# Gated linear attention on one core: products of even and odd heads issued in turn instead of one parity after the other

## The chip, the cores and the metric

The kernel runs on 1 core of one Trainium2 chip. The metric is the device time of one execution in microseconds (us); smaller is better. Engines are named as the profile names them: PE is TensorE (PEld its weight loads), DVE is VectorE, ACT is ScalarE, POOL is GpSimd, SP is SyncE.

## The reference, cut to what matters

The program is two transformer blocks in one launch. The change touches one stage of the first block: the output of the chunked gated linear attention (GLA). Per chunk of 64 tokens, per direction (forward and backward) and per head (4 heads, 64 key columns, 128 value columns):

```
q_dec = qi * exp(b);  k_inv = ki * exp(-b)
scores = where(mask, einsum("bihk,bjhk->bhij", q_dec, k_inv), 0)
o = einsum("bhij,bjhv->bihv", scores, vi) + einsum("bihk,bhkv->bihv", q_dec, state)
```

`o` of both directions is added, normalised per head and multiplied by a gate. All of it is float32.

## The kernel before

The kernel is written out by hand: each engine has its own list of stages, and between two stages stands a `fence` (L213), at which every engine waits until all have arrived. So a stage costs what its slowest chain costs, and stages do not overlap. The order of instructions on each engine is that of the Python loops; nothing reorders the program.

The stages around the change are, in order: `pe_dec` (decayed queries and keys, transposed), `pe_states` (L1056, the state of each of the 12 chunks, then `each_states`, whose recurrence L1079 runs on DVE alone), `pe_glao` (the stage that is changed), `pe_turn` (L1161, 32 transposes) and the output projection `pe_lin` (L506).

Sequence is 512 tokens, that is four token tiles t of 128 tokens (two chunks each). What `pe_glao` does for one tile, where par is the parity of the head (h = 2 q + par, q = 0, 1) and d the direction:

- **Scores** (L1098). `kiT` and `qdT` hold keys and queries with the 64 columns of even heads on partitions 0 to 63 and those of odd heads on partitions 64 to 127. So a score product contracts over 64 rows: the upper half of the array for par 0, the lower for par 1. Group g = 2 d + par writes bank g, two products (q) each; 8 products a tile.
- **Masks** (L1129, DVE). Four multiplications, one per group, take the scores out of banks 0 to 3 into `SM`.
- **Values** (L1110). For each head and direction one product over the whole array (128 rows, 128 columns): 8 a tile.
- **States** (L1116). For each head, direction and chunk c a product of the queries with the state before that chunk: 64 rows (those of par) by 64 output partitions (those of chunk c), 16 a tile, added to the values in bank 4 + 2 (t % 2) + par.
- **Copies** (L1144, ACT). One copy per parity takes the result out.

After the last copy DVE and ACT normalise (L834 and after) and the stage ends.

A float32 product is two records in the trace: the 8, 8 and 16 products of a tile are 16, 16 and 32 records of PE.

Of the kernel before, what the change touches and what calls it, by code (L numbers as in the profile page):

```python
# [39 lines left out]
DQ, DK, DV, GQ, GK, GV, GR, LRF, LRB, IN1 = 0, 512, 1024, 1536, 1792, 2048, 2560, 3072, 3088, 3104  # L40
# [69 lines left out]
def program(nc, I, out):  # L110
    ctx = ExitStack()
    with ctx:
# [11 lines left out]
        def sem(name):  # L124
            return ctx.enter_context(nc.semaphore(name))
# [19 lines left out]
        pjt = pj[:, :].rearrange("p (t n) -> p t n", t=TA)  # L145

        def bank(b, n=BANK):
            return ps[:, b * BANK:b * BANK + n]

        def C(at, n=P):  # L150
            return cst[:, at:at + n]
# [18 lines left out]
        mm_done, evac_a, evac_v = sem("mm_done"), sem("evac_a"), sem("evac_v")  # L170
# [651 lines left out]
        def rms_heads(eng, who, n, tiles, view, H, dh, gain, mul=1.0, at=0):  # L822

            nt = len(tiles)
            ss = st[:, 200:200 + nt * H]
            vv = st[:, 260:260 + nt * H]
            sd = st[:, 320:320 + nt * H]
            rr = st[:, 380:380 + nt * H]
            sq = [Z[:, at:at + H * dh], Z[:, at + 1024:at + 1024 + H * dh]]
            if who == "v":  # L830
                for i, t in enumerate(tiles):
                    v = view(t)
                    s3 = sq[i % 2].rearrange("p (h d) -> p h d", h=H)
                    nc.vector.tensor_tensor(s3, v, v, ALU.mult)  # L834
                    eng.drain()
                    nc.vector.tensor_reduce(ss[:, H * i:H * i + H], s3, AX, ALU.add)
                eng.drain()
                nc.vector.tensor_scalar(vv, ss, 1.0 / dh, EPS, ALU.mult, ALU.add).then_inc(var, 1)
                n["std"] += 1
                eng.wait_ge(std, n["std"])  # L840
                nc.vector.reciprocal(rr, sd)
                eng.drain()
                if mul != 1.0:
                    nc.vector.tensor_scalar(rr, rr, mul, None, ALU.mult)
                    eng.drain()
                for i, t in enumerate(tiles):
                    v = view(t)
                    nc.vector.tensor_tensor(v, v, rr[:, H * i:H * i + H].unsqueeze(2).broadcast_to([P, H, dh]), ALU.mult)
                if gain is not None:
                    eng.drain()  # L850
                    for i, t in enumerate(tiles):
                        v = view(t)
                        nc.vector.tensor_tensor(v, v, gain.unsqueeze(1).broadcast_to([P, H, dh]), ALU.mult)
            else:
                n["var"] += 1
                eng.wait_ge(var, n["var"])
                eng.activation(sd, vv, ACT.Sqrt).then_inc(std, 1)

        def hv(c0, H, dh):
            return lambda t: pjt[:, t, c0:c0 + H * dh].rearrange("p (h d) -> p h d", h=H)  # L860
# [29 lines left out]
        qdT = hT[:, 1536:3584].rearrange("p (t n) -> p t n", t=TL)  # L890
        kiT = hT[:, 3584:5632].rearrange("p (t n) -> p t n", t=TL)
        ex = [[Z[:, 3072 + 1536 * i + 512 * j:3584 + 1536 * i + 512 * j] for j in range(3)] for i in range(2)]
        qk = [Z[:, 6144 + 1024 * i:7168 + 1024 * i] for i in range(2)]
        DD = Z[:, 0:6144].rearrange("p (c d q n) -> p c d q n", c=12, d=2, q=2)
        SM = [[Z[:, 6144 + 1024 * i + 512 * d:6656 + 1024 * i + 512 * d] for d in range(2)] for i in range(2)]
        dec = st[:, 440:488]
        FWD = [8, 9, 10, 11] + list(range(8))
        BWD = [11, 10, 9, 8] + list(range(7, -1, -1))
# [186 lines left out]
        def plan_o(n):  # L1085
            return Plan(n, "vvvvaa" * TL)

        def pe_glao(pe, n):
            p = plan_o(n)
            for t in range(TL):  # L1090
                for g in range(4):
                    d, par = g // 2, g % 2
                    rs = slice(64 * par, 64 * par + 64)
                    if t:
                        pe.wait_ge(evac_v, p.val[6 * (t - 1) + g])
                    for q in range(2):
                        x = 256 * d + 128 * q
                        last = nc.tensor.matmul(bank(g)[:, 128 * q:128 * q + 128], kiT[rs, t, x:x + 128], qdT[rs, t, x:x + 128],  # L1098
                                                start=True, stop=True)
                    last.then_inc(mm_done, 1)  # L1100
                for par in range(2):
                    rs = slice(64 * par, 64 * par + 64)
                    pe.wait_ge(evac_v, p.val[6 * t + 2 + par])
                    if t >= 2:
                        pe.wait_ge(evac_a, p.val[6 * (t - 2) + 4 + par])
                    for q in range(2):
                        h = 2 * q + par
                        o = bank(4 + 2 * (t % 2) + par)[:, 128 * q:128 * q + 128]
                        for d in range(2):
                            nc.tensor.matmul(o, SM[t % 2][d][:, 128 * h:128 * h + 128], pjt[:, t, GV + 128 * h:GV + 128 * h + 128],  # L1110
                                             start=(d == 0), stop=False)
                        for d, order in enumerate((FWD, BWD)):
                            for c in range(2):
                                prev = order[order.index(2 * t + c) - 1]
                                x = 256 * d + 128 * q
                                last = nc.tensor.matmul(o[64 * c:64 * c + 64, :], qdT[rs, t, x + 64 * c:x + 64 * c + 64], DD[rs, prev, d, q, :],  # L1116
                                                        start=False, stop=(d == 1))
                    last.then_inc(mm_done, 1)

        def dve_glao(dve, n):  # L1120
            p = plan_o(n)
            for t in range(TL):
                if t >= 2:
                    dve.wait_ge(mm_done, p.done(6 * (t - 2) + 5))
                for g in range(4):
                    d, par = g // 2, g % 2
                    dve.wait_ge(mm_done, p.done(6 * t + g))
                    m = C(TRI[d]).unsqueeze(1).broadcast_to([P, 2, P])
                    nc.vector.tensor_tensor(SM[t % 2][d].rearrange("p (q a n) -> p a q n", q=2, a=2)[:, par],  # L1129
                                            bank(g, 256).rearrange("p (q n) -> p q n", q=2), m, ALU.mult).then_inc(evac_v, 1)  # L1130
            dve.wait_ge(evac_a, p.val[6 * (TL - 1) + 5])
            rms_heads(dve, "v", n, LAT, hv(DK, 4, 128), 4, 128, glag)
            dve.drain()
            n["a2v"] += 1
            dve.wait_ge(a2v, n["a2v"])
            for t in LAT:
                nc.vector.tensor_tensor(pjt[:, t, DK:DK + 512], pjt[:, t, DK:DK + 512], pjt[:, t, GR:GR + 512], ALU.mult)

        def act_glao(act, n):
            p = plan_o(n)  # L1140
            for t in range(TL):
                for par in range(2):
                    act.wait_ge(mm_done, p.done(6 * t + 4 + par))
                    act.activation(pjt[:, t, DK:DK + 512].rearrange("p (q a n) -> p a q n", q=2, a=2)[:, par],  # L1144
                                   bank(4 + 2 * (t % 2) + par, 256).rearrange("p (q n) -> p q n", q=2), ACT.Copy).then_inc(evac_a, 1)
            rms_heads(act, "a", n, LAT, hv(DK, 4, 128), 4, 128, glag)
            act.activation(pjt[:, 0:TL, GR:GR + 512], pjt[:, 0:TL, GR:GR + 512], ACT.Silu).then_inc(a2v, 1)
# [1383 lines left out]
        def _(pe):  # L2531
# [15 lines left out]
            pe_states(pe, n)  # L2547
            fence(pe, n)
            pe_glao(pe, n)
            fence(pe, n)  # L2550
            pe_turn(pe, n, KT, LAT, lambda k, t: pjt[:, t, 128 * k:128 * k + 128])
# [15 lines left out]
        def _(act):  # L2567
# [18 lines left out]
            each_states(act, n, "a")  # L2586
            fence(act, n)
            act_glao(act, n)
            fence(act, n)
            load_gate(act, 0, 2)  # L2590
# [20 lines left out]
        def _(dve):  # L2611
# [18 lines left out]
            each_states(dve, n, "v")  # L2630
            fence(dve, n)
            dve_glao(dve, n)
            fence(dve, n)
            each_turn(dve, n, "v", KT, LAT, hT_dst)
# [42 lines left out]
```

## Time and profile before

| what | value |
|---|---|
| median of 3 runs | 4378.2 us (4367.47, 4378.20, 4380.04) |
| the profiled execution, its own time | 4371.42 us |
| its span, first to last instruction | 4369.5 us |
| PE busy | 3613.9 us (83%) |
| weight loads (PEld) | 2471.3 us (57%) |
| DVE, ACT, POOL busy | 1530.4, 1050.7, 385.6 us |
| granted TensorE clock, mean | 0.901 |
| the stage of the change, first to last PE record | 575.9 to 621.5 us, 1.0% of the span |

The span is the time between the first and the last instruction of that one execution; its own time is 1.9 us longer. Busy time of an engine is the union of its records. PE records overlap, since products are pipelined: the time from the start of one to the start of the next is what a product costs in a stream, not its own length. The granted clock is given as a share: 1.00 is 2.4 GHz, 0.50 is 1.2 GHz.

### The profile page before, as it was taken

The numbers are of one execution on the slowest core, as the hardware profiler recorded it, in microseconds if no ns is written. First come the engines' busy times: TensorE is split into PE (matmuls) and PEld (weight loads), VectorE is DVE, ScalarE is ACT, GpSimd is POOL, SyncE is SP. The second block draws the span as 40 slices with busy tenths as digits, with TensorE's granted clock in tenths as the row PEclk, the third lists the DMA queues.
The fourth block names the chain that finished last, engine by engine and source line by source line (L and its number), as shares of the span: only waits on it lengthen the run. The fifth ranks groups of instructions, "written<-read, shape, count | busy, mean of one in ns | idle before, by whom it ended". The sixth has DMA issues, their size and how long they took to land. (4 is left out here: it accounts for less than half of the span.)

```text
span 4369.5 us, 42120 instructions
## 1 busy us (share of the span) xinstructions
PE 3613.9 (83%) x16571; PEld 2471.3 (57%) x16571; DVE 1530.4 (35%) x2853; ACT 1050.7 (24%) x1803; POOL 385.6 (9%) x227
## 2 busy tenths in 40 slices
PE   6997676688763988587999799999498778997998
PEld 2334553223322866466665388887386556655886
DVE  1115632000012546653112233333265662123444
ACT  1002411121214223233111322221323233113221
POOL 0000000100002231001110000000233001200000
PEclk9997767789986999888999899999799889998999
DMA  7772013799985210002112122121521003223222
GB/s 288 277 260 108 1 55 92 288 428 429 427 345 170 64 34 18 5 1 97 58 49 77 68 68 67 58 68 45 155 65 41 5 1 112 91 77 106 97 96 77
DMA packets 143631, 531.97 MB, mean 122 GB/s; under 512 B 8802, under 2 KB 47128, under 8 KB 120416
## 3 DMA queue, kind: packets, MB, share of 16 engines
q1 hardware_dynamic: 117184, 388.89, 23.6%
q0 software_dynamic: 19792, 102.32, 7.1%
q10 hardware_dynamic: 6480, 38.34, 2.2%
q8 instruction: 120, 1.97, 0.2%
q14 instruction: 55, 0.45, 0.0%
HBM read 486.74 MB, written 42.78 MB: 121 GB/s over the span
## 5 line engine op out<-in xcount | busy, mean ns | idle before, releaser
L506 PE MATMUL ps<-ring,hT 128*128 128x512 f32 (+1 forms) x1056 | 445.3, 581 | 13.0 <-DMA ring<-in_w_out_dram 10.2
L506 PEld LDWEIGHTS ps<-ring,hT 128*128 128x128 f32 x1056 | 199.1, 201 | 258.7 <-issue 255.5
L2177 PE MATMUL ps<-hT_hi,w_hi 128*128 128x512 f32 (+1 forms) x768 | 276.1, 359 | 20.5 <-DVE w_lo L2231 20.5
L1664 PE MATMUL ps<-wp_hi,hT_hi 128*128 128x512 f32 (+2 forms) x608 | 221.9, 365 | 67.5 <-POOL wp_lo L1643 67.5
L2177 PE MATMUL ps<-hT_hi,w_lo 128*128 128x512 f32 (+1 forms) x768 | 276.0, 359 | 0.0
L2177 PE MATMUL ps<-hT_lo,w_hi 128*128 128x512 f32 (+1 forms) x768 | 275.9, 359 | 0.0
L2183 PE MATMUL ps<-w_hi,h_lo 128*128 128x512 f32 x640 | 253.7, 396 | 0.0
L2183 PE MATMUL ps<-w_hi,h_hi 128*128 128x512 f32 x640 | 253.7, 396 | 0.0
L2183 PE MATMUL ps<-w_lo,h_hi 128*128 128x512 f32 x640 | 253.6, 396 | 0.0
L1664 PE MATMUL ps<-wm_hi,hT_hi 128*128 128x512 f32 x480 | 212.8, 443 | 37.4 <-POOL wm_lo L1947 37.4
L650 PE MATMUL ps<-pj,Z 128*128 128x64 f32 (+1 forms) x1856 | 237.2, 277 | 3.3 <-DVE hT L773 1.4
L650 PEld LDWEIGHTS ps<-pj,Z 128*128 128x128 f32 x1856 | 229.8, 198 | 5.1 <-issue 4.8
L1665 PE MATMUL ps<-wp_lo,hT_hi 128*128 128x512 f32 (+2 forms) x608 | 220.1, 362 | 0.0
L1666 PE MATMUL ps<-wp_hi,hm_lo 128*128 128x512 f32 (+2 forms) x608 | 220.1, 362 | 0.0
L2200 ACT ACTIVATE w_hi<-ring 128x2048 fp32r<-128x2048 f32 x64 | 122.0, 1909 | 328.4 <-PE ps L2183 326.8
L1439 PE MATMUL ps<-ring,Z 128*64 128x512 f32 x512 | 147.3, 740 | 54.2 <-ACT Z L1461 54.2
L1666 PE MATMUL ps<-wm_hi,hm_lo 128*128 128x512 f32 x480 | 189.1, 394 | 0.0
L1665 PE MATMUL ps<-wm_lo,hT_hi 128*128 128x512 f32 x480 | 188.3, 392 | 0.0
L2231 DVE TENSOR_TENSOR w_lo<-ring,w_hi 128x2048 fp32r<-128x2048 f32 x64 | 146.5, 2292 | 80.2 <-ACT w_hi L2200 80.2
L1947 POOL TENSOR_TENSOR wm_lo<-ring,wm_hi 128x2048 fp32r<-128x2048 f32 x20 | 91.0, 4556 | 905.5 <-ACT wm_hi L1938 905.5
L2177 PEld LDWEIGHTS ps<-hT_hi,w_hi 128*128 128x128 f32 x768 | 145.1, 189 | 45.3 <-issue 21.3
L599 PE MATMUL ps<-consts,pj 128*128 128x128 f32 (+1 forms) x224 | 43.8, 313 | 149.9 <-DVEq L213 98.2
(366 smaller groups left out, 6029.9 us busy)
## 6 DMA issues: line engine op xcount, KB each, us to landing
pj<-in_expert_w_up_dram SPq DMA_DIRECT2D x32, 2048.0 KB, 18.3
pj<-in_expert_w_down_dram SPq DMA_DIRECT2D x32, 2048.0 KB, 19.7
ring<-in_expert_w_gate_dram SPq DMA_DIRECT2D x32, 2048.0 KB, 16.0
ring<-in_ffn_w_dram SPq DMA_DIRECT2D x64, 1024.0 KB, 5.2
Z<-in_w_mod_dram POOLq DMA_DIRECT2D x24, 2048.0 KB, 8.0
ring<-in_w_in_dram SPq DMA_DIRECT2D x42, 1024.0 KB, 5.2
Z<-in_w_ada_dram POOLq DMA_DIRECT2D x8, 2048.0 KB, 7.9
ring<-in_w_in_dram SPq DMA_DIRECT2D x6, 2048.0 KB, 13.3
```

The costliest lines, as they stand in the source:

```text
L506: last = nc.tensor.matmul(bank(i % nb, w), lhs(k, t), s[:, k * w:k * w + w], start=(k == 0), stop=(k == nk - 1))
L599: last = nc.tensor.transpose(bank(7)[0:rows_, 128 * (t - ts[0]):128 * (t - ts[0]) + 128], src(side, t), ident)
L650: last = nc.tensor.matmul(bank(6, u["dv"]), ET[i % 2][:, 128 * t:128 * t + 128], u["v"](t), start=(t == u["keys"][0]), stop=(t == u["keys" ...
L1439: last = nc.tensor.matmul(bank(2 + m)[64 * x:64 * x + 64, :], xgT[:, k, 64 * x:64 * x + 64], mslot[2 * m + x][:, 512 * k:512 * k + 512], s ...
L1664: nc.tensor.matmul(out_, a_hi, b_hi, start=first, stop=False)
L1665: nc.tensor.matmul(out_, a_hi, b_lo, start=False, stop=False)
L1666: return nc.tensor.matmul(out_, a_lo, b_hi, start=False, stop=final)
L1947: pool.tensor_tensor(wm_lo[:, 2048 * y:2048 * y + 2048], mring[(3 * j + y) % 5], wm_hi[:, 2048 * y:2048 * y + 2048], ALU.subtract).then_in ...
L2177: last = nc.tensor.matmul(bank(i % 8, c1 - c0), W[a][:, k, :], r[:, k, c0:c1], start=(k == 0 and r is hhk and a == 0), stop=(k == KT - 1 a ...
L2183: last = nc.tensor.matmul(bank(i % 8), H1[hb % 2][a][:, k, P * what:P * what + P], W[b][:, k, :], start=(k == 0 and a == b), stop=(k == 3 ...
L2200: act.activation(WHI[x % 2], raw[x % 4], ACT.Copy).then_inc(w_hi_ok, 1)
L2231: nc.vector.tensor_tensor(WLO[x % 2], raw[x % 4], WHI[x % 2], ALU.subtract).then_inc(w_lo_ok, 1)
```

## The change

In `pe_glao` both loops over the parity move inwards. Scores: for each direction and q, the product of par 0 is followed by that of par 1 (they write banks 2 d and 2 d + 1), where before all of par 0 came first. Output: both parities of one q are worked together; first the four value products (two per parity), then the eight state products, in which par is the innermost loop. The number of products, their shapes, operands and banks are unchanged.

With that the semaphore waits change. PE waits for the masks of both parities before the first value product of a tile (`p.val[6 * t + 3]`, the last of the four masks, where par 0 waited for the third) and, from t = 2 on, for both copies of tile t - 2. DVE's mask of group g waits for the last score product of direction d (group 2 d + 1). Both of ACT's copies wait for the last product of the tile, where the copy of par 0 waited for the last one of par 0.

```diff
--- before.py
+++ after.py
@@ -1088,34 +1088,37 @@
         def pe_glao(pe, n):
             p = plan_o(n)
             for t in range(TL):
-                for g in range(4):
-                    d, par = g // 2, g % 2
-                    rs = slice(64 * par, 64 * par + 64)
+                for d in range(2):
                     if t:
-                        pe.wait_ge(evac_v, p.val[6 * (t - 1) + g])
+                        pe.wait_ge(evac_v, p.val[6 * (t - 1) + 2 * d + 1])
                     for q in range(2):
                         x = 256 * d + 128 * q
-                        last = nc.tensor.matmul(bank(g)[:, 128 * q:128 * q + 128], kiT[rs, t, x:x + 128], qdT[rs, t, x:x + 128],
-                                                start=True, stop=True)
-                    last.then_inc(mm_done, 1)
-                for par in range(2):
-                    rs = slice(64 * par, 64 * par + 64)
-                    pe.wait_ge(evac_v, p.val[6 * t + 2 + par])
-                    if t >= 2:
-                        pe.wait_ge(evac_a, p.val[6 * (t - 2) + 4 + par])
-                    for q in range(2):
+                        for par in range(2):
+                            rs = slice(64 * par, 64 * par + 64)
+                            last = nc.tensor.matmul(bank(2 * d + par)[:, 128 * q:128 * q + 128], kiT[rs, t, x:x + 128], qdT[rs, t, x:x + 128],
+                                                    start=True, stop=True)
+                            if q == 1:
+                                last.then_inc(mm_done, 1)
+                pe.wait_ge(evac_v, p.val[6 * t + 3])
+                if t >= 2:
+                    pe.wait_ge(evac_a, p.val[6 * (t - 2) + 5])
+                o = [[bank(4 + 2 * (t % 2) + par)[:, 128 * q:128 * q + 128] for q in range(2)] for par in range(2)]
+                for q in range(2):
+                    for par in range(2):
                         h = 2 * q + par
-                        o = bank(4 + 2 * (t % 2) + par)[:, 128 * q:128 * q + 128]
                         for d in range(2):
-                            nc.tensor.matmul(o, SM[t % 2][d][:, 128 * h:128 * h + 128], pjt[:, t, GV + 128 * h:GV + 128 * h + 128],
+                            nc.tensor.matmul(o[par][q], SM[t % 2][d][:, 128 * h:128 * h + 128], pjt[:, t, GV + 128 * h:GV + 128 * h + 128],
                                              start=(d == 0), stop=False)
-                        for d, order in enumerate((FWD, BWD)):
-                            for c in range(2):
-                                prev = order[order.index(2 * t + c) - 1]
-                                x = 256 * d + 128 * q
-                                last = nc.tensor.matmul(o[64 * c:64 * c + 64, :], qdT[rs, t, x + 64 * c:x + 64 * c + 64], DD[rs, prev, d, q, :],
-                                                        start=False, stop=(d == 1))
-                    last.then_inc(mm_done, 1)
+                    for d, order in enumerate((FWD, BWD)):
+                        for c in range(2):
+                            prev = order[order.index(2 * t + c) - 1]
+                            x = 256 * d + 128 * q
+                            for par in range(2):
+                                rs = slice(64 * par, 64 * par + 64)
+                                last = nc.tensor.matmul(o[par][q][64 * c:64 * c + 64, :], qdT[rs, t, x + 64 * c:x + 64 * c + 64],
+                                                        DD[rs, prev, d, q, :], start=False, stop=(d == 1))
+                                if (q, d, c) == (1, 1, 1):
+                                    last.then_inc(mm_done, 1)
 
         def dve_glao(dve, n):
             p = plan_o(n)
@@ -1124,7 +1127,7 @@
                     dve.wait_ge(mm_done, p.done(6 * (t - 2) + 5))
                 for g in range(4):
                     d, par = g // 2, g % 2
-                    dve.wait_ge(mm_done, p.done(6 * t + g))
+                    dve.wait_ge(mm_done, p.done(6 * t + 2 * d + 1))
                     m = C(TRI[d]).unsqueeze(1).broadcast_to([P, 2, P])
                     nc.vector.tensor_tensor(SM[t % 2][d].rearrange("p (q a n) -> p a q n", q=2, a=2)[:, par],
                                             bank(g, 256).rearrange("p (q n) -> p q n", q=2), m, ALU.mult).then_inc(evac_v, 1)
@@ -1140,7 +1143,7 @@
             p = plan_o(n)
             for t in range(TL):
                 for par in range(2):
-                    act.wait_ge(mm_done, p.done(6 * t + 4 + par))
+                    act.wait_ge(mm_done, p.done(6 * t + 5))
                     act.activation(pjt[:, t, DK:DK + 512].rearrange("p (q a n) -> p a q n", q=2, a=2)[:, par],
                                    bank(4 + 2 * (t % 2) + par, 256).rearrange("p (q n) -> p q n", q=2), ACT.Copy).then_inc(evac_a, 1)
             rms_heads(act, "a", n, LAT, hv(DK, 4, 128), 4, 128, glag)
```

In the built program, on PE, the first tile's scores, values and states stand as follows (L1098 scores, L1110 values, L1116 states, which after the change is L1118; a row with x4 is four products). Before:

```order
L1098 MATMUL ps<-hT 128x128 [waits stage_done]
L1098 MATMUL ps<-hT 128x128 x7
L1110 MATMUL ps<-pj,Z 128x128 [waits evac_v]
L1110 MATMUL ps<-pj,Z 128x128
L1116 MATMUL ps<-Z,hT 64x128 x4
L1110 MATMUL ps<-pj,Z 128x128 x2
L1116 MATMUL ps<-Z,hT 64x128 x4
L1110 MATMUL ps<-pj,Z 128x128 [waits evac_v]
L1110 MATMUL ps<-pj,Z 128x128
L1116 MATMUL ps<-Z,hT 64x128 x4
L1110 MATMUL ps<-pj,Z 128x128 x2
L1116 MATMUL ps<-Z,hT 64x128 x4
```

After the change, the same place:

```order
L1098 MATMUL ps<-hT 128x128 [waits stage_done]
L1098 MATMUL ps<-hT 128x128 x7
L1110 MATMUL ps<-pj,Z 128x128 [waits evac_v]
L1110 MATMUL ps<-pj,Z 128x128 x3
L1118 MATMUL ps<-Z,hT 64x128 x8
L1110 MATMUL ps<-pj,Z 128x128 x4
L1118 MATMUL ps<-Z,hT 64x128 x8
```

A tile's output was four blocks of two value products and four state products; it is now two blocks of four and eight, with one wait ahead of them instead of two.

The second place is the last tile's output and the start of the next stage, also on PE (`evac_a` counts ACT's copies, `evac_v` DVE's masks, L1161 is the first transpose of `pe_turn`, L1164 after the change). Before:

```order
L1110 MATMUL ps<-pj,Z 128x128 [waits evac_a,evac_v]
L1110 MATMUL ps<-pj,Z 128x128
L1116 MATMUL ps<-Z,hT 64x128 x4
L1110 MATMUL ps<-pj,Z 128x128 x2
L1116 MATMUL ps<-Z,hT 64x128 x4
L1110 MATMUL ps<-pj,Z 128x128 [waits evac_a,evac_v]
L1110 MATMUL ps<-pj,Z 128x128
L1116 MATMUL ps<-Z,hT 64x128 x4
L1110 MATMUL ps<-pj,Z 128x128 x2
L1116 MATMUL ps<-Z,hT 64x128 x4
L1161 MATMUL ps<-consts,pj 128x128 [waits stage_done]
```

After the change:

```order
L1110 MATMUL ps<-pj,Z 128x128 [waits evac_a,evac_v]
L1110 MATMUL ps<-pj,Z 128x128 x3
L1118 MATMUL ps<-Z,hT 64x128 x8
L1110 MATMUL ps<-pj,Z 128x128 x4
L1118 MATMUL ps<-Z,hT 64x128 x8
L1164 MATMUL ps<-consts,pj 128x128 [waits stage_done]
```

The wait for the copies of the tile two before stands once instead of once per parity, and the whole tile's products end together, right ahead of the fence.

## Rows read from the trace of the kernel before

**Rows 1.** The page: span, and busy time of PE and its weight loads.

```profile
span 4369.5 us, 42120 instructions
PE 3613.9 (83%) x16571; PEld 2471.3 (57%) x16571; DVE 1530.4 (35%) x2853; ACT 1050.7 (24%) x1803; POOL 385.6 (9%) x227
```

**Rows 2.** Timeline, 560 to 660 us: start, length (us), engine, line, out<-in, count, idle before.

```profile
575.89 2.24 PE L1098 MATMUL ps<-hT 64*128 64x128 f32 x16 [14.26 <-DVEq L213]
577.22 1.54 DVE L1129 TENSOR_TENSOR Z<-ps,consts 128x256 f32<-128x256 f32 x4 [1.46 <-PE ps L1098]
...
578.49 1.22 PE L1110 MATMUL ps<-pj,Z 128*128 128x128 f32 x4 [0.35 <-DVE Z L1129]
...
579.64 1.12 PE L1116 MATMUL ps<-Z,hT 64*64 64x128 f32 x8
...
580.68 1.22 PE L1110 MATMUL ps<-pj,Z 128*128 128x128 f32 x4
...
587.28 2.24 PE L1098 MATMUL ps<-hT 64*128 64x128 f32 x16
...
598.67 2.24 PE L1098 MATMUL ps<-hT 64*128 64x128 f32 x16
...
620.40 1.12 PE L1116 MATMUL ps<-Z,hT 64*64 64x128 f32 x8
621.56 0.38 ACT L1144 ACTIVATE pj<-ps 128x256 f32<-128x256 f32 x1 [4.02 <-PE ps L1116]
...
621.98 0.69 DVE L834 TENSOR_TENSOR Z<-pj 128x512 f32<-128x512 f32 x1 [9.05 <-ACT pj L1144]
```

**Rows 3.** Groups of the changed stage, shapes apart, 575.8 to 622 us: busy us, mean ns.

```profile
L1116 PE MATMUL ps<-Z,hT 64*64 64x128 f32 x128 | 17.9, 431 | 0.0
...
L1116 PEld LDWEIGHTS ps<-Z,hT 64*64 64x64 f32 x128 | 11.5, 215 | 3.6 <-issue 3.6
...
L1098 PEld LDWEIGHTS ps<-hT 64*128 64x128 f32 x64 | 7.8, 322 | 15.5 <-DVEq L213 14.5 <-issue 1.0
```

**Rows 4.** Transposes after the stage, L1161: 636.58 to 639.6 us, then from 640.3.

```profile
L1161 PE MATMUL ps<-consts,pj x16: 421/421/421, 636.4 to 639.6; 128*128 128x128 f32 x16
...
L1161 PE MATMUL ps<-consts,pj x13: 272/273/273, 640.1 to 641.4; 128*128 128x128 f32 x13
```

**Rows 5.** State products before the stage, L1056: 553.5 to 557.5 us, then 558.5 to 561.

```profile
L1056 PE MATMUL ps<-pj x74: 417/418/472, 553.2 to 557.4; 64*64 64x128 f32 x74
...
L1056 PE MATMUL ps<-pj x88: 269/269/321, 558.3 to 560.9; 64*64 64x128 f32 x88
```

**Rows 6.** Stretches: PE, PEld, DVE, ACT, POOL busy (count), granted clock, DMA share, GB/s.

```profile
552.50:558.00 5.50, 5.47 (x88) 5.47 (x90) 1.38 (x2) 1.19 (x2) 0.00 (x0) 0.50 0.01 1
558.10:561.80 3.70, 3.54 (x108) 3.29 (x102) 2.19 (x4) 2.39 (x4) 0.00 (x0) 1.00 0.02 4
575.90:621.50 45.60, 44.20 (x256) 34.10 (x256) 6.05 (x16) 2.69 (x7) 0.00 (x0) 0.50 0.00 1
622.00:636.00 14.00, 0.00 (x0) 0.00 (x0) 13.12 (x22) 4.66 (x4) 0.00 (x0) 0.50 0.00 0
636.10:639.90 3.80, 3.80 (x18) 3.80 (x19) 0.78 (x2) 1.20 (x2) 0.00 (x0) 0.50 0.64 253
640.00:641.70 1.70, 1.66 (x15) 1.42 (x13) 1.19 (x2) 1.03 (x2) 0.00 (x0) 1.00 0.10 39
...
808.00:817.20 9.20, 7.75 (x36) 2.76 (x36) 0.69 (x1) 0.60 (x1) 0.00 (x0) 1.00 1.00 429
820.90:827.60 6.70, 5.67 (x14) 1.71 (x16) 0.00 (x0) 2.26 (x4) 0.00 (x0) 0.50 0.99 418
```

**Rows 7.** Timeline of PE in the expert loop, 803 to 823 us.

```profile
808.76 0.75 PE L1444 MATMUL ps<-consts,Z 128*128 128x128 f32 x4 [0.78 <-DVE Z L1486]
810.19 7.09 PE L1452 MATMUL ps<-pj,Z 128*64 128x512 f32 x32 [0.69 <-ACT Z L1467]
817.21 1.16 PE L1430 MATMUL ps<-consts,Z 128*128 128x128 f32 x8
821.93 1.97 PE L1439 MATMUL ps<-ring,Z 128*64 128x512 f32 x4 [3.56 <-ACT Z L1461]
```

## The prediction

> **What bounds the kernel now.** I read the page first. PE is busy 83% of the span [rows 1], and all stages are separated by fences, so a stage is worth what its own chain takes, and nothing from outside it can hide or lose what is gained there. The changed stage is 45.6 us of 4369.5 [rows 1, 6], so even a third off it is 15 us, 0.35%. About 0.3% (13 us) is what a measurement of this kernel can tell from no change.
>
> The timeline shows who leads inside the stage [rows 2]. PE starts the scores at 575.89, DVE's four masks run from 577.22 to 578.76, PE goes on at 578.49 when the third mask is out, and then works without a wait to the next tile at 587.28. The third tile starts at 598.67. So a tile takes 11.39 us (587.28 - 575.89, and again 598.67 - 587.28): 2.60 from the scores to the first value product, and four blocks of 2.19 (580.68 - 578.49). PE sets the end; DVE matters in the 2.6 us only. The last products end at 621.52, ACT copies from 621.56, DVE goes on at 621.98.
>
> **What a product costs here.** In a stream of full-array records the transposes start one every 3.2 us / 15 = 0.213 us at granted clock 0.50, and every 1.3 us / 12 = 0.108 us at 1.00 [rows 4, 6]. The changed stage runs at 0.50 (1.2 GHz) from end to end [rows 6]. A burst of 8 state records lasts 1.12 us with the last record's 0.42 us, so eight start within 0.70 us: in pairs, 0.21 to 0.23 apart. Each pair is the two chunks of one parity: both column halves work, one row half is idle. The scores' 16 records last 2.24 us, so 16 start within 1.82 us; one after the other at 0.213 they would need 3.2. So in the scores **the two row halves already run side by side** although the program issues all of par 0 first: four records of one half are few enough for the other half's to start beside them. There the change finds nothing to gain.
>
> The Trainium skill (TensorE: Matmul & The Clock Gate, Part 3, The mechanism) says that matmuls start and end strictly in program order. This trace does not agree for tiles of different row halves: 16 score records start in 1.82 us. By the skill's rule the state products would gain little; that is the second rival below.
>
> **The change part by part, at clock 0.50.**
>
> 1. State products. Four at a time (two row halves by two column halves) is not seen in this stage. The nearest row is the stage before, L1056, the same shape 64*64 with both halves of rows: 74 records start in 4.2 us, four in 0.23 us, while its row half changes only every eight products [rows 5]. The other end is two at a time, as now. I take four at a time, since the rows are of the same form and clock and the new order alternates more finely.
> 2. Blocks. An old block of 2.19 us is 4 full-array records and 4 pairs, 8 x 0.213 = 1.71, and 0.48 for two changes of form with their slow first records. A new block is 8 full-array records and 4 quads, 12 x 0.213 = 2.56, plus the same 0.48, plus 0.02 for the two further starts in the first quad: 3.06. Two new blocks are 6.12 against 8.76 to 8.79.
> 3. The later wait. PE waits for the fourth mask instead of the third. The masks end at 578.76, and with the 0.05 that PE needs behind a mask it starts at 578.82 instead of 578.49: +0.33 a tile, 2.93 in all. That DVE's first mask waits for both groups of a direction costs nothing, since both end together. The two waits that PE's scores lose cost nothing either: those masks are out some 8 us before.
> 4. A tile: 2.93 + 6.12 = 9.05, saves 2.34; four tiles 9.4.
> 5. The tail. Both copies now follow the last product, where one was done long before: one copy of 0.38 us more, less what two back to back overlap, +0.35. For tiles 0 to 2 the copies have a whole tile's time.
>
> Sum at 0.50: -9.4 + 0.35 = **-9.0 us**.
>
> 6. **The clock.** Look at what PE did before each rise near here [rows 6]. At L1056, quads of state products from 552.5: at 558.0 the clock went from 0.50 to 1.00, after 5.5 us. At the transposes, full array without a gap: 0.50 up to 639.9, 1.00 from 640.0, after 3.8 us. The changed stage has PE occupied 44.20 of 45.60 us and stays at 0.50 throughout. What sets it apart from the other two is not idleness but the half array in its state products (17.9 us of its records [rows 3]) and the doubled number of form changes. The new block is all full array or quads, with half as many changes, so it is nearer to the two stretches that rose than to the one that did not; I take it that the clock rises. Bounds: never, or as early as 6 us into the stage.
>
> The Trainium skill (the same page, Part 1, What's actually happening) says that sustained activity releases the throttle. If activity means that PE is occupied, the clock should be up in this stage already; the row does not agree, with 44.20 us busy at 0.50. By that reading the change would do nothing for the clock and the sum would stay at -9.0; that is the first rival.
>
> What 1.00 gives: 12 pitches of 0.108 are 1.30 instead of 2.56. The 0.48 shrinks to between 0.24 and 0.48; one part of it, the longer first record of a 64*64 group, is 0.05 at either clock (472 against 418, 321 against 269 [rows 5]), so I take 0.38, a block of 1.68. Ahead of the blocks DVE gets its first group earlier: three pitches (0.32) and the shorter record (0.42 to 0.27, 0.15) are 0.47, and the masks stay as they are: 2.93 becomes 2.46. A tile takes 2.46 + 3.36 = 5.8 instead of 9.05. When it rises: 5.5 us behind the first block's start at 2.9, so about 8.4 us into a stage of 36.2. The other 27.8 us shrink by 5.8/9.05 to 17.8: -10.0. It holds: in the expert loop PE is idle for 0.78 and 0.69 us within 1.5 us and the clock stays at 1.00; an idle time of 3.56 brings 0.50 [rows 6, 7]. In the new tile the wait for the masks is about 1 us.
>
> Behind PE's end nothing changes: 14.0 us of DVE and ACT with PE idle [rows 6], after which the transposes start cold as they do now, whatever the clock was.
>
> **Sum: -9.0 - 10.0 = -19.0 us.** The profiled execution took 4371.4 (span 4369.5 and 1.9 around it); it becomes 4352.4. It lies 6.8 below the median of the three runs; from the median the forecast is 4378.2 - 19.0 = 4359.2 us.
>
> **The rivals.**
>
> - *The clock stays at 0.50.* Quads work, but score gaps and form changes keep it down. For it: the stage never rose once in 45.6 us. Against it: L1056. Time: 4378.2 - 9.0 = 4369. Chance 0.15. If it rises but falls at each mask wait, the time is between, near 4364 (chance 0.04).
> - *The quads do not form*: the change does not do what it says, products start in program order or the second row half waits. Then 8 state products take some 9 pitches instead of 4: +1.07 a block, 4.13, two of them 8.26 against 8.76, less the 0.33 of the wait: about 0.2 a tile gained, 0.35 lost at the end, clock unchanged. Time 4378. Chance 0.06.
> - *Slower: weight loads come into the open at each change of row half.* 32 score and 64 state products now alternate. If PE loaded weights ahead only within a half, each would expose a load of 0.322 or 0.215 us [rows 3]: 10.3 + 13.8 = 24.1, with 1.7 for the later waits and 2.2 back from 16 fewer changes of form, +23.6: 4402. It decides from 0.16 us per product (96 x 0.16 = 15). Against it: L1056 and the scores change halves with no such gap. Chance 0.03.
>
> **How the numbers follow.** Forecast 0.72. Its own spread: the rise at 6 or 10 us gives 0.7 either way, a fast tile of 5.4 to 6.3 gives 1.3, and the three runs lie 12.6 us apart, which moves a median by some 5. So it lies between about 4350 and 4368, and beyond 13 us in about 0.85 of it; the cold rival is at 9 us and passes in a fifth of its cases, the one between in half. Faster: 0.61 + 0.03 + 0.02 = 0.66. Slower: the last rival and stray medians, 0.04. Same: 0.30. The range reaches past the cold rival: 4349 to 4373.
>
> **What would show it.** Right: 64 + 64 + 128 PE records still; bursts of 16 state records within 1.15 us at clock 0.50, and within about 0.65 at 1.00; first value product 2.9 us after the first score; granted clock 0.50 for the first 6 to 10 us and 1.00 to the end of PE's work; stage 26 us instead of 45.6; two ACT copies back to back. Step 6 is wrong if the clock reads 0.50 and the stage takes 36; step 1 if a burst of 16 takes over 1.8 us; all of it if any other stage has moved by more than a microsecond.

## The result and the profile after

| | before | changed |
|---|---|---|
| median, us | 4377.36 (4 runs, 4367.47 to 4380.04) | 4348.06 (4 runs, 4347.45 to 4350.69) |
| ratio | | 0.9938, 95% interval 0.9921 to 0.9956 |
| span of the profiled execution, us | 4369.5 [rows 1] | 4346.5 |
| PE busy, us | 3613.9 [rows 1] | 3584.8 |
| stage, first score to first transpose, us | 60.2 | 40.0 |
| of it PE's part, first score to last product, us | 45.6 | 25.1 |

Faster, by about half a percent. The four first runs of before lie high among those taken later: beside the experiments below the same kernel ran 29, 23 and 13 times, with medians of 4366.5, 4368.1 and 4365.8. One further execution of it, one of twelve in the first experiment, took 15760.96 us at a mean granted clock of 0.214 and is left out of that experiment's median and ratio. A second measurement of the changed kernel, against the last of these, gave 4343.17 and a ratio of 0.9958 (0.9943 to 0.9973). Both intervals lie clear of 1. The second, with more runs of before, is the better guide to the size: 0.0042 x 4366 = 18 us, where the stage gained 20.2.

The page of the changed kernel, answering to [rows 1]:

```profile
span 4346.5 us, 42118 instructions
...
PE 3584.8 (82%) x16571; PEld 2457.1 (57%) x16571; DVE 1530.4 (35%) x2853; ACT 1050.2 (24%) x1803; POOL 385.7 (9%) x227
```

The timeline of the changed stage, answering to [rows 2] (L1118 is the old L1116, L1132 the old L1129, L1147 the old L1144, L1164 the old L1161):

```profile
572.52 2.08 PE L1098 MATMUL ps<-hT 64*128 64x128 f32 x16 [14.25 <-DVEq L213]
573.89 1.54 DVE L1132 TENSOR_TENSOR Z<-ps,consts 128x256 f32<-128x256 f32 x4 [1.50 <-PE ps L1098]
...
575.48 2.07 PE L1110 MATMUL ps<-pj,Z 128*128 128x128 f32 x8 [0.88 <-DVE Z L1132]
...
577.49 1.13 PE L1118 MATMUL ps<-Z,hT 64*64 64x128 f32 x16
...
578.55 1.45 PE L1110 MATMUL ps<-pj,Z 128*128 128x128 f32 x8
...
579.93 0.67 PE L1118 MATMUL ps<-Z,hT 64*64 64x128 f32 x16
...
580.53 1.16 PE L1098 MATMUL ps<-hT 64*128 64x128 f32 x16
580.75 0.66 ACT L1147 ACTIVATE pj<-ps 128x256 f32<-128x256 f32 x2 [22.34 <-PE ps L1118]
...
582.79 1.16 PE L1110 MATMUL ps<-pj,Z 128*128 128x128 f32 x8 [1.10 <-DVE Z L1132]
...
584.47 1.16 PE L1110 MATMUL ps<-pj,Z 128*128 128x128 f32 x8
...
586.16 1.16 PE L1098 MATMUL ps<-hT 64*128 64x128 f32 x16
...
612.53 5.74 PE L1164 MATMUL ps<-consts,pj 128*128 128x128 f32 x32 [14.90 <-DVEq L213]
```

Two speeds are to be seen in one stage here. The first block runs at the low clock: from 575.48 to 578.55, 3.07 us, against two old blocks of 2.19. Its burst of 16 state records is 1.13 us long; the old burst of eight was 1.12 [rows 2]. In the middle of the second block the same lines become shorter: 2.07 to 1.16, 1.13 to 0.67. From there a block takes 1.68 (584.47 - 582.79) and a tile 5.63 (586.16 - 580.53). The granted clock says why:

```profile
572.60:579.20 6.60, 5.72 (x43) 4.87 (x44) 1.51 (x4) 0.00 (x0) 0.00 (x0) 0.50 0.01 2
579.30:597.60 18.30, 14.87 (x215) 12.21 (x213) 4.25 (x12) 1.98 (x6) 0.00 (x0) 1.00 0.00 1
597.70:612.40 14.70, 0.00 (x0) 0.00 (x0) 13.11 (x22) 5.35 (x6) 0.00 (x0) 0.57 0.00 0
```

(Stretches as in [rows 6], granted clock third from the end.) It was 0.50 for the first 6.7 us and 1.00 to the end of PE's work. DVE's part behind it is unchanged, 13.11 against 13.12 us. So the span's gain of 23.0 is 20.2 in the stage; 3.4 us had been gained before it began (572.5 against 575.9), and a little was lost behind it. Neither of these two is in the change: the same stage starts at 576.30 in a second trace of before and at 570.15 in one in which only its scores differ.

### The profile page after: what moved, and what is told of

Read it like the earlier page. It is cut to its first block and busy times, and to the rows that moved or that the text cites. A ratio compares the mean times of both kernels' runs of the same rounds, so it can differ in the third digit from the quotient of the medians.

```text
span 4346.5 us, 42118 instructions
## 1 busy us (share of the span) xinstructions
PE 3584.8 (82%) x16571; PEld 2457.1 (57%) x16571; DVE 1530.4 (35%) x2853; ACT 1050.2 (24%) x1803; POOL 385.7 (9%) x227
```

## The experiments

Stage lengths are from the first score product to the first transpose of the next stage, PE's part to the end of the last product; both are differences of starts and ends in each run's timeline.

### The kernel before, again

No edit.

> The kernel before, once more, for its spread. Theory (the stage alone changed): median 4377 +- 3, stage from first score to first transpose 60.2 us as in its first trace. Rival (the 9 us beyond the stage are real and sit in later stages): also 4377, but then this second trace shows the later stages as slow as or slower than the first. If instead its own runs wander by 10 us and more, the 9 us are scatter of before.

Median 4365.42 (11 runs), ratio 0.9998 (0.9982 to 1.0013). Stage 60.2 us, PE's part 45.6, tiles of 11.39, as in its first trace:

```profile
576.40:621.90 45.50, 44.10 (x256) 34.01 (x256) 6.04 (x16) 2.69 (x7) 0.00 (x0) 0.50 0.00 1
```

The stage does not scatter; the total does, from 4353.65 to 4378.57 over the 29 runs beside it. The median expected, 4377, was not met. So the 9 us that the first result gained beyond the stage (29.3 less 20.2) lie within the scatter of before.

Part of where that scatter sits can be read from the pages. This trace and the next one, whose changed stages are within 0.2 us of each other, span 4367.2 and 4350.4 us; PE is busy 3613.5 and 3594.9 us, and the mean granted clock is 0.901 and 0.905. So the 17 us are in PE's busy time, and the longer one has the lower clock. What sets the clock apart in two executions was not tested.

### Only the scores alternate

```diff
-                for g in range(4):
-                    d, par = g // 2, g % 2
...
+                for d in range(2):
...
                     for q in range(2):
                         x = 256 * d + 128 * q
+                        for par in range(2):
```

The score loops and DVE's wait are as in the change, the output as before.

> Only the scores alternate, the output stays one parity after the other. Theory (the row halves of the scores already ran side by side): stage 60.2 us within 0.5, clock 0.50 in it, total 4377 +- 3. Rival (alternation itself is what pays, here too): each tile 0.2 to 1.5 us less, stage 54 to 59 us. Rival (the denser scores raise the clock): stage 45 to 50 us.

Stage 60.4 us, PE's part 45.8, tiles of 11.43, total 4366.2, ratio 1.0004 (0.9992 to 1.0015).

```profile
570.15 2.08 PE L1098 MATMUL ps<-hT 64*128 64x128 f32 x16 [14.25 <-DVEq L213]
572.78 1.22 PE L1111 MATMUL ps<-pj,Z 128*128 128x128 f32 x4 [0.55 <-DVE Z L1130]
```

The 16 score records are packed 0.16 us closer than in [rows 2] (2.08 against 2.24), but the first value product starts 2.63 us behind the first score instead of 2.60: DVE's four masks, not PE, set this piece. Nothing gained, clock 0.50 throughout, as expected; the total of 4377 that was expected with it was the old reference again.

### Only the output works both parities together

The opposite half: output loops and waits as in the change, score loops as before.

> Only the output works both parities together, the scores stay one parity first. Theory: the whole gain, stage 40.0 us within 0.8 and total as the changed kernel, 4348 +- 3. Rival (the scores' order carries part): stage 41 to 46 us.

Stage 39.9 us, total 4346.24, ratio 0.9955 (0.9938 to 0.9972). The clock rose at 6.7 us here too:

```profile
573.90:580.50 6.60, 5.92 (x43) 5.07 (x44) 1.51 (x4) 0.00 (x0) 0.00 (x0) 0.50 0.01 2
580.70:598.80 18.10, 15.10 (x214) 12.45 (x213) 4.24 (x12) 1.97 (x6) 0.00 (x0) 1.00 0.00 1
```

All of the gain is in the output loops.

### New blocks, but one parity after the other inside them

```diff
-                    for d, order in enumerate((FWD, BWD)):
-                        for c in range(2):
-                            prev = order[order.index(2 * t + c) - 1]
-                            x = 256 * d + 128 * q
-                            for par in range(2):
-                                rs = slice(64 * par, 64 * par + 64)
+                    for par in range(2):
+                        rs = slice(64 * par, 64 * par + 64)
+                        for d, order in enumerate((FWD, BWD)):
+                            for c in range(2):
+                                prev = order[order.index(2 * t + c) - 1]
+                                x = 256 * d + 128 * q
```

> Blocks as in the change (four value products, then eight state products), but inside a block the four state products of par 0 come first, then the four of par 1. Theory A (a row half queues a few records and the other half's start beside them, as in the scores): the burst of 16 state records still takes 1.13 us at clock 0.50, stage 40 us within 1. Theory B (strict alternation is needed): the burst takes about 1.9 us at 0.50, 8 bursts +6.8 us, and the clock may stay low: stage 44 to 57 us.

```profile
577.46 2.07 PE L1110 MATMUL ps<-pj,Z 128*128 128x128 f32 x8 [0.88 <-DVE Z L1132]
579.46 1.15 PE L1118 MATMUL ps<-Z,hT 64*64 64x128 f32 x16
580.53 2.07 PE L1110 MATMUL ps<-pj,Z 128*128 128x128 f32 x8
582.54 0.93 PE L1118 MATMUL ps<-Z,hT 64*64 64x128 f32 x16
583.40 1.16 PE L1098 MATMUL ps<-hT 64*128 64x128 f32 x16
```

The burst of 16 takes 1.15 us at clock 0.50 with eight records of one half issued first: theory A. At 1.00 it is 0.68 against 0.67. The stage took 41.0 us, 1.0 more, because the clock rose 8.6 us into it instead of 6.7; its fast tiles are 5.65 and 5.73. That the later rise is not due to the grouping is shown by the run with a delay below: it has the changed kernel's own order, its clock rose at 8.6 too, and PE's part took 26.0 us there against 26.1 here. Total 4350.47, ratio 0.9965 (0.9953 to 0.9977). So the fine alternation of the row halves, which names this change, is not what pays. What pays is that both parities stand between the same two changes of form. (A change of form is the switch between records of shape 128*128 and of 64*64.)

### The old order, with work on PE ahead of the stage

```diff
             pe_states(pe, n)
+            pe.wait_ge(evac_a, n["a"])
+            pe.wait_ge(evac_v, n["v"])
+            for _ in range(56):
+                nc.tensor.transpose(bank(0, P), ident, ident)
```

The transposes' results are not used. They are to run while DVE works the recurrence (L1079) and PE is idle; the two waits are for the copies of the stage before.

> The old order, with 56 full-array transposes of a constant on PE in its idle time before the stage (results unused), so that the stage starts at clock 1.00. Theory (clock and overlap are two separate terms): a block 1.24 and a tile 7.4 us at 1.00, stage 60.2 - 15.8 = 44.4 us if the clock holds through it. Rival (the old order cannot hold 1.00): the clock falls within the stage, stage 50 to 60 us.

```profile
561.45 6.30 PE L2551 MATMUL ps<-consts 128*128 128x128 f32 x56 [0.88 <-DVE Z L1070]
574.82 1.60 PE L1098 MATMUL ps<-hT 64*128 64x128 f32 x10 [7.07 <-DVEq L213]
```

(This view ended at 576, which is why the scores show 10 records.) A miss of the set-up: a transpose is one record, not two, so the 56 were done 7.07 us before the stage. The clock was at 1.00 while they ran and had fallen when the stage began:

```profile
561.50:567.70 6.20, 6.20 (x56) 6.01 (x56) 5.82 (x21) 0.00 (x0) 0.00 (x0) 1.00 0.01 3
574.90:620.40 45.50, 44.10 (x256) 34.02 (x256) 6.05 (x16) 2.69 (x7) 0.00 (x0) 0.50 0.00 1
```

Stage 60.2, not the 44.4 expected; total 4364.01 (ratio 0.9990, 0.9979 to 1.0001). The same transposes ahead of the new order:

> The new order with the same 56 transposes ahead. Theory: all four tiles at the fast tile's 5.7 us, stage 40.0 - 3.4 = 36.6 us, total 3 us below the changed kernel. Rival (the clock was not what made tiles 2 to 4 faster): no change of the stage, 40.0.

Stage 39.9 us, not 36.6, clock up at 6.5; total 4346.23, ratio 0.9954 (0.9939 to 0.9969). As both stages began at 0.50, neither run tests what it was built for. With 118 in place of 56, the old order first:

> The old order again, now with 118 transposes ahead (56 took 6.3 us and ended 7 us before the stage, so that the clock was down again when it began); 118 should last 13 us and end right before it. Theory (clock and overlap are separate terms): first tile about 7.4 us at clock 1.00, stage 44.4 us if the clock holds to its end. Rival (the old order cannot hold 1.00): a fast first tile, then 0.50 and tiles of 11.4 us, stage 50 to 58 us.

```profile
558.69 13.07 PE L2551 MATMUL ps<-consts 128*128 128x128 f32 x118 [0.89 <-DVE Z L1070]
572.05 1.26 PE L1098 MATMUL ps<-hT 64*128 64x128 f32 x16 [0.29 <-DVEq L213]
574.01 0.71 PE L1110 MATMUL ps<-pj,Z 128*128 128x128 f32 x4 [0.69 <-DVE Z L1129]
574.65 0.65 PE L1116 MATMUL ps<-Z,hT 64*64 64x128 f32 x8
575.23 0.71 PE L1110 MATMUL ps<-pj,Z 128*128 128x128 f32 x4
...
578.91 1.26 PE L1098 MATMUL ps<-hT 64*128 64x128 f32 x16
```

```profile
562.00:575.00 13.00, 12.02 (x116) 11.47 (x116) 10.74 (x37) 0.00 (x0) 0.00 (x0) 1.00 0.00 0
576.00:600.00 24.00, 21.48 (x224) 16.56 (x224) 4.29 (x13) 3.13 (x9) 0.00 (x0) 1.00 0.00 1
```

The clock is up when the stage begins and stays at 1.00 to its end, in the old order. A block is 1.22 us, a tile 6.86 (578.91 - 572.05), the stage 42.0 instead of 60.2: **18.2 us by the clock alone**, with not one product of the stage moved. That is 2.4 us more than the 44.4 expected would have given: the blocks are as forecast (1.22 against 1.24), but the first value product starts 1.96 us behind the first score. Total 4344.75, ratio 0.9957 (0.9943 to 0.9971), the same as the changed kernel's. And the new order behind the same 118:

> The new order with the same 118 transposes. Theory: the first tile is as fast as the others, 5.6 to 5.7 us instead of 8.0, stage 37.6 us, total 2.4 us below the changed kernel. Rival (the transposes cost their own time on a chain that sets the stage before): total no lower.

```profile
570.97 1.16 PE L1098 MATMUL ps<-hT 64*128 64x128 f32 x16 [0.29 <-DVEq L213]
573.29 1.16 PE L1110 MATMUL ps<-pj,Z 128*128 128x128 f32 x8 [1.17 <-DVE Z L1132]
...
574.98 1.16 PE L1110 MATMUL ps<-pj,Z 128*128 128x128 f32 x8
...
576.67 1.16 PE L1098 MATMUL ps<-hT 64*128 64x128 f32 x16
```

First tile 5.70, stage 37.7, as expected. Total 4336.9 (4 runs), ratio 0.9944 (0.9924 to 0.9964): 6.3 below the changed kernel's second median where the stage gives 2.3, the rest within the scatter of totals.

The stage in all four cases:

| stage, us | clock 0.50 at its start | clock 1.00 at its start |
|---|---|---|
| old order | 60.2 (stays at 0.50) | 42.0 (stays at 1.00) |
| new order | 40.0 (rises at 6.7) | 37.7 (stays at 1.00) |

At an equal clock of 1.00 the new order is worth 4.3 us: a new block takes 1.69 where two old ones take 2.45, and of the 6.1 us that eight of them gain, 1.4 go to the later first value product of each tile (2.32 against 1.96) and 0.3 to the two copies at the end. The other 15.9 of the change's 20.2 depend on where the old order finds the clock.

### Scores one tile ahead

PE issues the scores of tile t + 1 before the output of tile t; the waits follow that order.

```diff
+        GO = [("s", 0)] + [x for t in range(TL) for x in ([("s", t + 1)] if t + 1 < TL else []) + [("o", t)]]
...
-            for t in range(TL):
+            for kind, t in GO:
```

> The new order, with the scores of tile t+1 issued ahead of the output of tile t, so that DVE's masks run beside PE's output. Theory: three of four mask waits (1.1 to 1.3 us each) go, one stays at the first tile: stage 40.0 - 3.6 = 36.4 us, total 4344. Rival (PE then waits elsewhere, on banks or copies): under 1 us gained.

```profile
584.31 1.16 PE L1111 MATMUL ps<-hT 64*128 64x128 f32 x16
...
585.40 1.16 PE L1124 MATMUL ps<-pj,Z 128*128 128x128 f32 x8
```

Between the scores and the next output PE no longer waits (1.09 us from start to start, where the changed kernel needs 2.26). Stage 35.6 us, 4.4 less where 3.6 was expected; the clock also rose earlier, about 5.9 us into the stage. Total 4342.62, ratio 0.9952 (0.9939 to 0.9964). With the 118 transposes:

> New order, scores one tile ahead, 118 transposes ahead of the stage. Theory: both gains add, every tile but the first 4.5 us from the start, stage 33 to 34 us, total about 4339, below both kernels. Rival (with the clock up PE waits for DVE's masks or ACT's copies again): stage 35 us or more.

Stage 33.6 us, the scores of the fourth tile starting 4.47 us behind those of the third: both gains add in the stage, nearly (4.4 and 2.3 alone, 6.4 together). The span of its profiled execution is the lowest seen, 4329.2, but the median of 6 runs is 4342.74 (4331.12 to 4352.56), ratio 0.9955 (0.9939 to 0.9971). 6.4 us off the stage are within the scatter of these totals, so that either of these two beats the changed kernel is shown for the stage and not for the whole.

### A delay of the same size behind the stage

```diff
+            for _ in range(27):
+                dve.drain()
+                nc.vector.tensor_tensor(Z[:, 2048:2560], pjt[:, 0, GR:GR + 512], pjt[:, 1, GR:GR + 512], ALU.mult)
```

> The changed kernel with 27 extra VectorE multiplications behind the stage's last one (unused results), which delay all that follows by about 20 us, as much as the stage gained. Theory (later stages just shift): total is the changed kernel's plus 20, 4368. Rival (the 9 us beyond the stage hang on when the later stages start): total 4377.

```profile
582.30 2.07 PE L1110 MATMUL ps<-pj,Z 128*128 128x128 f32 x8
584.30 0.94 PE L1118 MATMUL ps<-Z,hT 64*64 64x128 f32 x16
```

The stage became 61.6 us, 21.6 more than the changed kernel's. Of that 20.7 are the delay (PE is idle for 35.60 us behind its last product, where the changed kernel has 14.90), and 0.9 come from the clock: up to its last product the stage is the changed kernel's own, and still the clock rose 8.6 us into it and not 6.7, so that nearly all of the second block, above, is slow.

Total 4368.78, ratio 1.0009 (0.9993 to 1.0025), 12 runs from 4360.62 to 4403.85. The median is the one of a mere shift, 4347 and 21.6 (4347 being about what the changed kernel and its close kin measured). But the interval goes from 4365 to 4379 us at the 4368.08 of before, and so the rival's 4377 is not excluded. The run does not settle what the later stages do; that the 9 us were scatter rests on the three later medians of before.

### The changed kernel, again

> The changed kernel once more, for its spread and a second trace of its stage. Theory: median 4347 +- 2, ratio to before 0.9955, stage 40.0 us, up to 1.5 us more or less by the moment at which the clock rises. Rival (the first result's 0.9938 is the true ratio): 4340.

4343.17 (6 runs), 4 below the expected, ratio 0.9958 (0.9943 to 0.9973) as expected. Stage 40.0 us, clock up at 6.6, tiles of 7.97, 5.64 and 5.70. With the clock up at 6.5 to 6.7 the stage repeats to 0.2 us; in the delayed run, up at 8.6, it took 0.9 more. Totals of one kernel do not repeat to 5.

## Why the prediction was right, point by point

- **Scores** (nothing to gain). Right. Alternating them alone left the stage at 60.4 us. The Trainium skill (TensorE: Matmul & The Clock Gate, Part 3, The mechanism) says that matmuls start strictly in program order. By that rule the halves issued in runs of eight records could hardly overlap, and such a burst would take some 1.7 us (an estimate: six pitches of 0.213 and a last record of 0.42); here it took 1.15, so the trace does not agree. The prediction drew one thing too many from the rule, though: products that alternate can overlap and still start in program order, so the rule never spoke against the quads of the new order, and the second rival does not follow from it.
- **Step 1 and 2, quads and blocks.** Right: block 3.07 against 3.06 forecast, burst 1.13 against 1.15. The second rival would have shown 4.13. How the 1.31 us a pair of old blocks loses divides between the row halves and the halved changes of form was only calculated (four pitches of 0.213, 0.85, and one 0.48); no run took one away alone.
- **Step 3 and 5, later wait and tail.** 2.96 us to the first value product against 2.93. The two copies are 0.66 us together, 0.28 more than one, and from the last product to the first transpose it is 0.3 more; 0.35 was forecast.
- **Step 6, the clock.** Right in kind: it rose and held through waits of about 1.1 us, while the old order, entered at 0.50, never rose in four traces. The step named two differences, full-array or quad records and half as many changes of form; no run has one without the other, so which of them raises the clock is not shown, and that it would rise at all was a judgement from two neighbouring stretches. In the six traces of the new blocks that began at 0.50 without the scores ahead it rose after 6.7, 6.7, 6.6, 6.5, 8.6 and 8.6 us, where 8.4 was taken and 6 to 10 given.
- **The fast tile** came to 5.63 to 5.70 against 5.8. The term that was off is the lead-in: 2.26 to 2.33 measured, 2.46 forecast. The block was 1.68 as forecast.
- **Sum.** Stage -20.2 against -19.0: 1.1 us from the earlier rise and the shorter lead-in. The part at 0.50 comes to -8.8 from measured pieces (an estimate: four tiles of 2.96 + 2 x 3.07 against 11.39, less 0.3), where -9.0 was forecast. The measured median, 4348.06, stands 0.9 below the range's low end, while its ratio, applied to the 4378.2 from which the forecast started, gives 4351.1. The weak step was the reference, not the mechanism: three runs of before were taken for its middle, and their median lay some 12 us above the 4366.5 of the next 29. From 4366.5 the same sum gives 4347.5.
- **The slower rival**, weight loads in the open: no sign. With both row halves alternating, 16 score records start within 1.66 us (2.08 less 0.42), closer than before. Its price was loose: at the 0.24 a change of step 2, 16 fewer changes give back 3.8 us, not 2.2.
- **"Nothing from outside can hide or lose what is gained there"**, the reason given for looking at the stage alone, is wrong. The fences keep the work of stages apart, but not the clock: with 118 transposes ahead of it the old stage takes 42.0 us instead of 60.2, and most of what the change gains there was to be had outside the stage.
- **A sign that misfired.** All of the prediction was to be wrong if another stage moved by more than a microsecond. The stages ahead took 3.4 us less, but they vary by more than that without any edit to them (the stage starts between 570.15 and 576.30 us in the traces of the old order), so this sign could not have told anything.
- What the prediction did not see is how lopsided its two terms are. It priced overlap at 9.0 and clock at 10.0, in that order. In the other order, clock first, they are 18.2 and 4.3 (42.0 to 37.7), less 2.3 for the first tile and a half that the change still runs at 0.50.

## What to carry to other kernels

Read the granted clock of each stage before counting products: a stage in which PE is occupied 97% of the time can stand at 0.50 for its whole length, and then an edit of its order can be worth more by the clock than by the time it takes off the products (15.9 against 4.3 us here). If PE is idle ahead of such a stage, filling that idle time up to the stage's start may give nearly the same without touching the stage (18.2 of 20.2 us here). To overlap the two row halves it was enough that both stood in one run of the same form, eight records of each; the order within the run mattered by less than 0.05 us a burst.

## What was not expected of the hardware

- The same instructions in the same order took 45.6 us of PE at 0.50 and 27.4 at 1.00, and each clock lasted to the end: which one the old order gets is settled by what PE did right before. 56 transposes that ended 7.07 us ahead had no effect, since the clock, 1.00 while they ran, was back at 0.50; 118 that ended 0.29 us ahead were worth 18.2 us.
- Eight records of one row half, issued first, do not hold back the other half's: the burst of 16 took 1.15 us against 1.13 when they alternate. In both traces the records start in fours, 0.21 us apart.
- The total of one kernel on one core wandered by 25 us (0.6%) over 29 runs, while the old stage repeated to 0.1 us in three traces, and the changed one to 0.2 or, with a later rise of the clock, 0.9 us. For a change of this size the stage's own length is the sharper measurement. In the 29 runs the longer ones have the lower mean granted clock (0.905 at 4353.65 and 4356.00 us, 0.899 and 0.900 at 4377.60 and 4378.57); what moves it was not tested.
